# Gathering the next expert's tokens in three parts around an expert's last turn and last down product

## The reference, cut to what matters

```
logits = h @ router_w + router_b                 # 256 tokens, 8 experts
top_w  = softmax(the two largest logits)         # each token goes to 2 experts
for e in 8 experts:
    y += combine[:, e] * (silu(h @ w_gate[e]) * (h @ w_up[e])) @ w_down[e]
x = x + gate_f * y
```

## Time and profile before

| what | value |
|---|---|
| time, median of 3 runs | 2566.53 us (2561.96 to 2567.74) |
| time of the profiled execution | 2569.26 us |
| its span in the trace | 2567.5 us |
| mean granted clock of TensorE | 0.985 |
| PE busy | 2448.9 us, 95% of the span |
| DVE, ACT, POOL busy | 652.6, 417.2 and 52.8 us |
| read from HBM | 614.69 MB, mean 240 GB/s |

### The profile page before, as it was taken

How to read it: one execution, slowest core, us unless ns; L and a number is a source line. 1 busy time by engine, 2 the same in 40 slices (tenths; PEclk the granted TensorE clock), 3 DMA queues, 4 the chain that set the end, 5 groups by cost and what they waited for, 6 DMA issues and landing times.

```text
span 2567.5 us, 27861 instructions
## 1 busy us (share of the span) xinstructions
PE 2448.9 (95%) x11154; PEld 1545.7 (60%) x11155; DVE 652.6 (25%) x1444; ACT 417.2 (16%) x1051; POOL 52.8 (2%) x108
## 2 busy tenths in 40 slices
PE   8999999999999999999999989978999989989997
PEld 4666466656564666666777755448994544445443
DVE  0353210011542144463344451101001101011101
ACT  1243010000530133101321111101001101001101
POOL 0000000000000000000000000000000000000000
PEclk9999999999999999999999989998998999999999
DMA  6323253434223778335664558997775999869980
GB/s 241 134 99 123 106 186 141 155 119 153 101 92 123 286 295 317 147 111 229 275 282 177 201 238 351 425 427 306 271 277 219 425 426 426 319 253 399 425 317 22
DMA packets 78667, 617.33 MB, mean 240 GB/s; under 512 B 5936, under 2 KB 6064, under 8 KB 38624
## 3 DMA queue, kind: packets, MB, share of 16 engines
q1 hardware_dynamic: 73616, 558.39, 55.5%
q0 software_dynamic: 4656, 56.47, 5.6%
q10 hardware_dynamic: 288, 0.90, 0.1%
HBM read 614.69 MB, written 1.05 MB: 240 GB/s over the span
## 4 chain that ended last, share of the span: by engine, by line
PE 87%; DMA 8%; DVE 2%; issue 1%; ACT 1%; POOL 0%; ACTq 0%; DVEq 0%; SPq 0%; POOLq 0%
PE G L2122 9%; PE S L2434 8%; DMA big<-in_moe_pack 7%; PE G L1849 6%; PE S L2432 6%; PE G L1887 5%; PE S L2115 4%; PE T L2115 4%; PE G L2448 4%; PE G L2069 3%; PE S L2324 3%; PE T L2324 3%; PE G L2347 3%; PE G L2446 3%; PE S L2498 2%; PE G L2081 2%
## 5 line engine op out<-in xcount | busy, mean ns | idle before, releaser
L2432 PE MATMUL S<-big,hT 128*64 128x256 f32 x2240 | 271.4, 385 | 40.3 <-DMA big<-in_moe_pack 33.1
L2432 PEld LDWEIGHTS S<-big,hT 128*64 128x64 f32 x2240 | 159.7, 137 | 148.8 <-issue 65.1
L2122 PE MATMUL G<-big 128*128 128x512 f32 x512 | 222.2, 592 | 0.0
L1752 DVE TENSOR_TENSOR probs<-S,probs 128x128 f32<-128x128 f32 (+2 forms) x105 | 35.5, 338 | 692.7 <-ACT probs L1077 692.6
L2434 PE MATMUL S<-big,hT 128*128 128x512 f32 x448 | 201.3, 592 | 0.8 <-issue 0.8
L1849 PE MATMUL G<-big,hT 128*128 128x372 f32 x512 | 163.0, 481 | 12.1 <-DMA big<-in_proj_pack 12.1
L1887 PE MATMUL G<-big,hT 128*128 128x384 f32 x512 | 171.0, 488 | 0.0
L2122 PEld LDWEIGHTS G<-big 128*128 128x128 f32 x512 | 97.2, 190 | 116.0 <-issue 115.3
L1849 PEld LDWEIGHTS G<-big,hT 128*128 128x128 f32 x512 | 98.3, 192 | 75.4 <-issue 14.4
L2446 PE MATMUL G<-big,pT 128*64 128x512 f32 x560 | 132.3, 593 | 8.7 <-ACT pT L1082 8.7
L2434 PEld LDWEIGHTS S<-big,hT 128*128 128x128 f32 x448 | 82.8, 190 | 95.2 <-issue 95.2
(11 more groups left out here) (360 smaller groups left out, 2735.2 us busy)
## 6 DMA issues: line engine op xcount, KB each, us to landing
big<-in_moe_pack SPq DMA_DIRECT2D x112, 2048.0 KB, 18.2
big<-in_moe_pack SPq DMA_DIRECT2D x112, 1024.0 KB, 15.6
big<-in_w_ff SPq DMA_DIRECT2D x32, 2048.0 KB, 8.4
big<-in_ada_pack POOLq DMA_DIRECT2D x24, 2048.0 KB, 14.0
big<-in_ffn_pack SPq DMA_DIRECT2D x11, 3072.0 KB, 14.5
big<-in_gate_pack SPq DMA_DIRECT2D x16, 1536.0 KB, 6.2
big<-in_proj_pack SPq DMA_DIRECT2D x16, 1488.0 KB, 6.4
big<-in_branch_heads SPq DMA_DIRECT2D x6, 2048.0 KB, 7.8
```

What stands on the lines that cost most here:

```text
L2122: return mm(G[j][:, :], hid[:, c % 2, f, b * P:(b + 1) * P], w[:, f, half * 512:(half + 1) * 512], start=(c == 0 and f == 0), stop=(c == 7 ...
L2432: ins = mm(S[s % 2][f * FEW:(f + 1) * FEW, 0:SEQ], hTe[:, k, 0:FEW], wt[:, k, f * SEQ:(f + 1) * SEQ], start=(k == 0), stop=(k == KD - 1))
```

## The change

On PE, the gather of a narrow or 128-wide expert (`expert`) is cut in three. The matmuls of k = 0 to 3 stay where the gather stood, then comes the last turn, then the matmuls of k = 4 and 5, then the last down product, then those of k = 6 and 7. `gather` signals `gath_mm` twice, behind k = 3 and behind k = 7, wherever it is called. ACT waits for the first signal and DVE for the second. On ACT the last `hidden_turned` stands ahead of the inputs. On DVE the inputs stand behind the product `ye` and ahead of the adds. At the start of an expert of at most 128 tokens PE waits for ACT's half of the inputs alone, and for DVE's half ahead of k = 4 of the first step. The wide body's order stays as it is, save for the two signals. The number of matmuls is the same.

```diff
@@ ScalarE: inputs @@
-                        act.wait_ge(mm_done.sem, count)
-                        for k in range(KD // 2):
+                        act.wait_ge(mm_done.sem, 2 * count - 1)
+                        for k in range(KH):
@@ ScalarE: expert @@
                             sigmoids(e, last, 1, w)
+                            hidden_turned(e, last, 1, w)
                             inputs(gath_mm, e + 2, hTe_act, G[0])
-                            hidden_turned(e, last, 1, w)
@@ VectorE: inputs @@
-                        dve.wait_ge(mm_done.sem, count)
-                        for k in range(KD // 2, KD):
+                        dve.wait_ge(mm_done.sem, 2 * count)
+                        for k in range(KH, KD):
@@ VectorE: expert @@
                         if w <= P:
-                            inputs(gath_mm, e + 2, hTe_dve, G[1])
                             dve.wait_ge(down_mm.sem, e * ESTEPS + (FSTEPS + ESTEPS))
...
                                 ins.then_inc(ye_dve.sem, 1)
+                            inputs(gath_mm, e + 2, hTe_dve, G[1])
                             return add_results(e, SCAT)
@@ TensorE: gather @@
-                    def gather(banks, done, c0=0, n=P):
-
-                        for k in range(KD):
+                    def gather(banks, done, c0=0, n=P, k0=0, k1=KD):
+
+                        for k in range(k0, k1):
                             for b in range(NB):
-                                ins = mm(banks[k // 4][:, k % 4 * P:k % 4 * P + n], ...)
-                        ins.then_inc(done.sem, 1)
+                                ins = mm(banks[k // KH][:, k % KH * P:k % KH * P + n], ...)
+                            if k % KH == KH - 1:
+                                ins.then_inc(done.sem, 1)
@@ TensorE: gate_up @@
                         for k in range(KD):
+                            if k == KH and s == 0:
+                                pe.wait_ge(hTe_dve.sem, e + 1)
@@ TensorE: expert @@
-                        pe.sem_inc(xgath_mm.sem, 1)
-                        gathered(e + 1)
+                        pe.sem_inc(xgath_mm.sem, 2)
+                        pe.wait_ge(hTe_act.sem, e + 1)
                         gate_up(e, 0, w)
...
                         pe.wait_ge(sel_ok.sem, e + 2)
-                        gather(G, gath_mm)
+                        gather(G, gath_mm, k1=KH)
                         turn_hidden(e, ESTEPS - 1, w)
+                        gather(G, gath_mm, k0=KH, k1=6)
                         down(e, ESTEPS - 1, w)
+                        gather(G, gath_mm, k0=6)
                         pe.sem_inc(edn_done.sem, 1)
```

More of the change, by code:

```diff
@@ L2391, in _ @@
                     mm(S[0][:, 32:40], ones, chosen[:, 1, :], start=False, stop=True).then_inc(rank_mm.sem, 1)
-                    def gather(banks, done, c0=0, n=P):
-                        for k in range(KD):
+                    def gather(banks, done, c0=0, n=P, k0=0, k1=KD):
+                        for k in range(k0, k1):
                             for b in range(NB):
-                                ins = mm(banks[k // 4][:, k % 4 * P:k % 4 * P + n], xn[:, b, k * P:(k + 1) * P], sel[:, b, c0:c0 + n], start=(b == 0), stop=(b == NB - 1))
-                        ins.then_inc(done.sem, 1)
+                                ins = mm(banks[k // KH][:, k % KH * P:k % KH * P + n], xn[:, b, k * P:(k + 1) * P], sel[:, b, c0:c0 + n], start=(b == 0), stop=(b == NB - 1))
+                            if k % KH == KH - 1:
+                                ins.then_inc(done.sem, 1)
                     def gathered(count):
```

## The result

The kernel after takes 2546.96 us (median of 4 runs, 2546.12 to 2550.36); the kernel before took 2567.14 beside it (4 runs). The ratio is 0.9926, interval [0.9914, 0.9939]: 20 us less by the medians, 0.7% by the ratio. The forecast was 2555.0, its range began at 2549.5.

What follows compares the result with a forecast made beforehand. PE was taken as the bound (87% of the chain of waits), except where weight loads limit e1 and e4. Savings of 3.6 + 3.7 + 2.8 + 1.4 = 11.5 us from the median 2566.53 gave 2555.0, range 2549.5 to 2562.5.

Steps and rivals of the forecast that it cites:

- the end of e5: 128-wide end of e5: the 5.03 us branch starts 1.4 us sooner, so 1.4 us saved, bounds 0.7 and 2.8.
- more branches miss: Rival: long branches at the starts of e3, e5 and e7, 5.0 to 6.2 us each; chance 0.10.
- The clock: Rival: more PE idle before e6 brings low-clock stretches, 1.7 to 3.4 us more, or 1.7 less; chance 0.12.
- Part 1: Starts of e0 and e3: PE waits for ACT's half only, idle of 1.85 and 1.78 us goes, 3.6 saved.
- part 2: Narrow ends: 1.2 us saved at e4 and e6, 1.3 at e1, sum 3.7.
- The added wait: Narrow ends: the spreading's second half waits for DVE's later inputs, so the gain is 1.2 us, not 2.6.
- Part 3: 128-wide ends: e7's last add moves with the spreading, 2.8 us saved, bounds 1.4 and 3.7; e5 counted at 1.4.
- The DMA: Ends of e0 and e3: the 1.2 us saved is swallowed, as e1 and e4 run on a full DMA.
- e1 and e4 stay near 92.6 us: Sign of being right: windows of e1 and e4 keep their length, with DMA share 1.0.

Runs made afterwards that it cites:

- starts_only: Kernel before with only the half signals and PE's two waits, gather left whole: ratio 0.9956 against the kernel before.
- after_banks: Kernel after with the spreading's second half in other banks (S[1], T[0]) and no added wait at the ends: 2542.27 us, ratio 0.9908 against the kernel before.
- e0: Not a run: an expert with a narrow end, ahead of e1; PE's idle before its first step was 1.85 us in the kernel before.
- banks_wide_hint: Kernel after with other spreading banks, no added wait, plus a hint in narrow experts for the branch to the wide body: 2540.19 us, ratio 0.9896.
- after_late: Kernel after with the gather's third part (k = 6 and 7) ahead of the last down product: ratio 0.9956 against the kernel before.
- fill_start: Kernel before with four extra matmuls (16 PE instructions) in 128-wide experts, behind step 0's down product, 130 us ahead of the end: ratio 0.9994.
- fill_start_one: Kernel before with 4 extra PE instructions in 128-wide experts, behind step 0's down product: 2564.25 us in one run, e5-to-e6 branch 5.14 us.
- after_two: Kernel after with the gather in two parts and DVE's inputs ahead of its wait for the down product: ratio 0.9941 against the kernel before.
- before_again: Kernel before, unchanged, profiled once more: 2564.21 us.
- after_again: Kernel after, unchanged, profiled once more: 2550.12 us.
- e7: Not a run: the last expert, 128-wide; from its first gather matmul the last add starts 11.73 us later in the kernel after, 14.61 before.

## Why the prediction missed

**The step that failed is the end of e5**, the passage from "At e5 the next body is not in reach of the branch, so PE stands in L496 for 5.03 us" to "I count 1.4, not 2.8". It took the stall as a fixed price behind a moving start. The start moved much as forecast: the branch begins 9.49 us behind the gather instead of 11.10, so 1.6 sooner. But the branch then took 0.47 us. The stall went, so the whole 2.87 us by which the spreading starts sooner counted, and 3.37 more (7.00 to 3.63). The bound given for this step, 2.8, was too tight: a branch that cost 5.03 us and whose fetch the profile doesn't explain should have been bounded by its disappearance. The rival "more branches miss" looked at the slow side of exactly this lever only. That it can go either way with small edits is shown: nine kernels have it long, eight short. The other terms together were near: 12.1 us in the first pair of profiles and 8.9 in the second, where 10.1 were forecast. That this kernel falls on the short side was luck: nothing in the change aims at it, and why it does stays open.

**The clock** was priced right, at 1.7 us, and its falling away was named with no chance of its own. e6 took 1.9 us less. The stretch at 0.50 stands in e6 in nine of the ten profiles with the long branch and in none of the ten with the short one. It goes with the stall, but the stall alone doesn't bring it: starts_only has a branch of 4.97 us and e6 at full clock.

**Part 1** was right (1.9 us of idle time at each start against 1.85 and 1.78), and so was **part 2** in size, step by step. But the experiments correct its reading. The text gave the 1.2 us of a narrow end to the three parts; starts_only has 1.4 there without them. I had left out that, with the gather in one piece, ACT's early inputs free it for the copy of the turned features. **The added wait** was priced at 1.4 us (a gain of 1.2 instead of 2.6). It costs 1.7 us at a narrow end, and nothing at e5: shown by after_banks. **Part 3**'s 2.8 came out at 2.9.

**The DMA** swallowed the narrow ends of e0 and e3 as forecast, but the sign given for it, "e1 and e4 stay near 92.6 us", was wrong. Where the end before them is shorter and the loads are the limit, e1 and e4 must get longer by as much, and they did: 93.7 and 93.8 us. In after_banks, whose narrow ends are another 1.7 us shorter, they take 95.4. The end of e0 or e3 and the next expert together take 103.2 to 103.4 us in every kernel but banks_wide_hint, which has 104.7 with its low clock.

What of the branch stays open: why a kernel has it long. It is not long by the length of the body that it leads back over. In the kernel before, the closing branches of the six other experts took 0.23 to 0.39 us, five of them over narrow bodies, longer than e5's (some 1270 instructions of PE are recorded in e4 and 858 in e5), and one over the wide body. That of e4:

```profile
L496 PEldq COMPARE_BRANCH  x1: 230/230/230, 2142.5 to 2142.5; - x1
```

Shown is when its page of instructions comes. In the transfers of the kernel before (queue, packets, MB, share of 16 engines) from 2294.0 to 2302.3 there is no packet of instructions, and from 2302.3 to 2303.0 there is one:

```profile
q1 hardware_dynamic: 183, 1.65, 53.9%
```

```profile
q8 instruction: 1, 0.02, 7.9%
```

In the kernel after one stands between 2284.1 and 2284.8, 3 us ahead of the branch at 2287.3:

```profile
q8 instruction: 1, 0.02, 8.1%
```

In all ten profiles with the long branch it starts 2.8 to 3.2 us behind the moment at which `ye` lets PE go on. after_late tells that moment apart from the branch's start. There the added wait puts the branch (second row) 1.5 us behind the release, and the stall is shorter by 1.0 to 1.4 us, 3.97; the packet (first row, window 2295.5 to 2296.0) comes 3.0 us behind the release at 2292.52 and only 1.6 behind the branch:

```profile
q8 instruction: 1, 0.02, 11.1%
```

```profile
L496 PEldq COMPARE_BRANCH  x1: 3972/3972/3972, 2294.0 to 2294.0; - x1
```

The starts of the packets in e5 say a little more. In the kernel before they are 2147.9, 2172.4, 2212.3 and 2253.7, then 2302.4, so the last comes 48.7 us behind the fourth. In the kernel after they are 2137.0, 2161.4, 2201.0 and 2243.0, then 2284.2, so it comes after 41.2 us, much like the one before it (42.0). The distance is 40.7 to 41.9 us in six of the other seven kernels with the short branch, and 46.3 to 48.9 in eight of the nine with the long one; fill_start (46.9) and fill_start_one (37.0), with fillers early in the body, fall out. So the packet looks like the next one of a row, on time in the short kernels and held up in the long ones. This is a reading of the distances; no run tested it.

So the fetch seems to be asked for ahead of the branch, by something that in some kernels stands behind the wait for `ye` and in others ahead of it. What that is was not found. Excluded as the sole cause, by runs: two instructions of place, the order of the gather, DVE's inputs, the hint's place, and chance in one profile. 16 instructions ahead of the last down product (near or 130 us ahead) shorten it, 4 don't, and 16 behind it don't. Not excluded is an edge of the pages of instructions that lies 5 to 16 instructions away in the kernel before; a shift of the whole program by more than two instructions, with nothing added in the bodies, was not run.

The rule of the Trainium skill named in the prediction (page Runtime: NRT & Kernel Launch, section Instruction fetch mechanics, a taken branch outside the current two pages stalls) agrees with the long branches, 4.93 to 5.33 us. It doesn't tell the short ones: the same branch over the same kind of body took 0.47 to 0.63 us in eight kernels, and in the kernel before itself six of the seven closing branches took 0.23 to 0.39.

## What to carry to other kernels

Bound a long taken branch by its full price on both sides, since edits of a few instructions near it can switch it off or on; profile each variant at that branch before comparing variants by their times. Signal a producer's halves before cutting it in parts: at the narrow ends the half signals alone gave 1.4 us, the three parts alone 1.0. Where the loads are the limit, look for a saved microsecond in the next window too, which gets longer by as much. And where a reused buffer forces a wait at the head of a queue, look for another buffer first: other banks for the spreading were worth 1.7 us at each narrow end.

## What the runs showed of the hardware

- The closing branch from e5 to e6 took 0.47 to 0.63 us or 4.93 to 5.33, nothing between but the 3.97 where the branch stood 1.5 us behind the release. Net of the spreading that covers it, the stall is worth 3.2 to 3.6 us (6.83 to 7.19 from the spreading's start to the next step, against 3.63), and some 1.6 to 2.2 more with the 3.4 us of low clock behind it (3.9 in after_two, where that stretch is 6.8 us). The other closing branches of the kernel before took 0.23 to 0.39.
- From 2040 to 2147 us the kernel before has no packet on PE's instruction queue: all of e4, a narrow body behind a narrow body, ran without one. e5 behind it had four.
- A hint in the body of e1, 9.3 us ahead of the branch at the loop's head, cut it from 6.38 to 0.37 us (one kernel, one profile). Why e1 and e4 then had stretches at a clock of 0.50 is open.
- The granted clock differs between profiles of one and the same kernel. The window 651.9 to 655.3, far ahead of the experts, has it at 0.50 in the first profile of the kernel before and at 1.00 in its second, before_again (first row and second row). The kernel after is the other way round: 1.00 in the first profile (third row), and a stretch at 0.50 at 651.1 in after_again. This stretch comes with one of 6.8 instead of 3.4 us near 1416, and with a later start of e0's gather: 1536.6 to 1537.1 us in the seven profiles that have it, 1533.0 to 1534.6 in the eleven that have none so early (two have one at 120 us, and start at 1536.3 and 1537.4). So the 3.0 us ahead of e0's gather belong to the execution. Distances behind it carry some of the clock too, as e0's gather shows.

```profile
651.90:655.30 3.40, 3.40 (x17) 2.28 (x16) 1.29 (x2) 0.00 (x0) 0.00 (x0) 0.50 0.45 188
```

```profile
651.90:655.30 3.40, 3.05 (x27) 2.44 (x24) 3.16 (x6) 1.43 (x6) 0.00 (x0) 1.00 0.22 94
```

```profile
651.90:655.30 3.40, 3.05 (x27) 2.41 (x24) 2.81 (x5) 1.09 (x4) 0.00 (x0) 1.00 0.34 145
```
